# Between two sublayers: the second half's root steps among the first half's features, the last tile's sums behind the next unit's first product

## The reference

```
x = x + 0.5 * rmsnorm(swiglu(rmsnorm(x, g0)), g1)
x = x +       rmsnorm(mixer (rmsnorm(x, g2)), g3)
x = x + 0.5 * rmsnorm(swiglu(rmsnorm(x, g4)), g5)
```

## Time and profile before

| | |
|---|---|
| three runs | 2788.54, 2783.35, 2790.81 us (median 2788.54) |
| profiled execution | 2786.83 us, its span 2785.2 us |
| PE busy | 2673.0 us, 96% |
| DVE / ACT / POOL busy | 1274.3 / 855.1 / 427.5 us |
| chain that ended last | PE 90%, DVE 5% |
| root of half 1 and diagonal, third turn | 1376.60 to 1379.91 us |

### The profile page before, as it was taken

How to read it: one execution, slowest core, us unless ns; L and a number is a source line. 1 busy time by engine, 2 the same in 40 slices (tenths; PEclk the granted TensorE clock), 3 DMA queues, 4 the chain that set the end, 5 groups by cost and what they waited for, 6 DMA issues and landing times.

```text
span 2785.2 us, 52286 instructions
## 1 busy us (share of the span) xinstructions
PE 2673.0 (96%) x20733; PEld 2511.4 (90%) x20733; DVE 1274.3 (46%) x2112; ACT 855.1 (31%) x1415; POOL 427.5 (15%) x616
## 2 busy tenths in 40 slices
PE   7999999999888999999999999999999889999998
PEld 6999998977444999999899999899999878999998
DVE  5444226554544444432444442468435555544423
ACT  2222223233432332222332232334333233322221
POOL 3000003011443100000100000255144442000001
PEclk9999999999999999999999999999989999999999
DMA  4233322222997222332123333133110114233321
GB/s 116 83 90 88 102 75 69 77 68 72 332 339 264 61 83 84 90 103 84 56 85 89 89 97 94 44 84 83 46 36 1 31 47 129 77 89 90 103 84 43
DMA packets 397671, 263.03 MB, mean 94 GB/s; under 512 B 10954, under 2 KB 370583, under 8 KB 397497
## 3 DMA queue, kind: packets, MB, share of 16 engines
q1 hardware_dynamic: 386012, 223.03, 27.4%
q0 software_dynamic: 11536, 38.28, 4.1%
HBM read 251.71 MB, written 9.56 MB: 94 GB/s over the span
## 4 chain that ended last, share of the span: by engine, by line
PE 90%; DVE 5%; issue 1%; ACT 1%; DMA 1%; POOL 1%; SPq 0%; DVEq 0%; POOLq 0%; ACTq 0%
PE ps L486 67%; PE ps L472 5%; PE ps L2247 2%; PE ps L2268 1%; PE ps L1369 1%; PE ps L2265 1%; PE ps L1381 1%; PE ps L1421 1%; PE ps L500 1%; PE ps L1312 1%; PE ps L1330 1%; PE ps L527 1%; PE ps L1313 1%; PE ps L2231 1%; PE ps L2489 1%
## 5 line engine op out<-in xcount | busy, mean ns | idle before, releaser
L464 DVE TENSOR_TENSOR w_lo<-w_raw,w_hi 128x1024 fp32r<-128x1024 f32 (+1 forms) x314 | 419.8, 1337 | 957.9 <-ACT w_hi L457 956.6
L486 PE MATMUL ps<-hd_hi,w_hi 128*128 128x272 f32 x3712 | 774.7, 290 | 6.0 <-DVE w_lo L464 6.0
L486 PE MATMUL ps<-hd_lo,w_hi 128*128 128x272 f32 x3712 | 767.9, 288 | 0.0
L486 PE MATMUL ps<-hd_hi,w_lo 128*128 128x272 f32 x3712 | 764.1, 287 | 0.0
L457 ACT CAST w_hi<-w_raw 128x1024 fp32r<-128x1024 f32 (+1 forms) x314 | 351.1, 1118 | 1088.6 <-PE ps L486 1023.0
L486 PEld LDWEIGHTS ps<-hd_hi,w_hi 128*128 128x128 f32 x3712 | 581.4, 189 | 14.7 <-issue 14.3
L486 PEld LDWEIGHTS ps<-hd_lo,w_hi 128*128 128x128 f32 x3712 | 584.7, 189 | 0.0
L486 PEld LDWEIGHTS ps<-hd_hi,w_lo 128*128 128x128 f32 x3712 | 582.3, 189 | 0.0
L967 POOL TENSOR_TENSOR xT<-xT,rstd_rows 128x272 f32<-128x272 f32 x96 | 81.0, 871 | 1709.4 <-DVE rstd_rows L992 1709.4
L486 PE MATMUL ps<-h_hi,w_hi 128*128 128x272 f32 x1232 | 255.3, 289 | 0.0
L486 PE MATMUL ps<-h_lo,w_hi 128*128 128x272 f32 x1232 | 254.7, 288 | 0.0
(11 more groups left out here) (500 smaller groups left out, 3175.6 us busy)
## 6 DMA issues: line engine op xcount, KB each, us to landing
w_raw<-in_ffn_w_gate_dram SPq DMA_DIRECT2D x88, 512.0 KB, 3.8
w_raw<-in_ffn_w_up_dram SPq DMA_DIRECT2D x88, 512.0 KB, 3.8
w_raw<-in_ffn_w_down_dram SPq DMA_DIRECT2D x64, 704.0 KB, 4.5
k_pages<-in_cache_a_k_dram SPq DMA_DIRECT2D x128, 256.0 KB, 4.6
v_pages<-in_cache_a_v_dram POOLq DMA_DIRECT2D x128, 256.0 KB, 4.5
w_raw<-in_c_w_in_dram SPq DMA_DIRECT2D x33, 512.0 KB, 4.1
w_raw<-in_ab_w_in_dram SPq DMA_DIRECT2D x25, 512.0 KB, 3.9
w_raw<-in_ab_w_out_dram SPq DMA_DIRECT2D x8, 512.0 KB, 3.7
```

Of the source, the lines that this page charges most:

```text
L464: e.tensor_tensor(w_lo[:, n % 2, 0:nk * P], raw[:, n % RAW, 0:nk * P], w_hi[:, n % 2, 0:nk * P].bitcast(F32), ALU.subtract).then_inc(sem(" ...
L486: mm = e.matmul(ps[:, bank + h, 0:TH], w, x[:, k0 + k, half(h)], start=first and k == 0 and w is wh and x is x_hi, stop=last and k == nk - ...
```

## The change

1. `pe_y` ends with its products unless it is the last sublayer. The last sums of half 1, with their wait, become `pe_last_sums`, which `pe_head` of the next sublayer calls right after the three products of feature 0, half 0, of the first unit.
2. `pe_rows` of half 1 moves from behind feature 4 to behind feature 5.
3. ACT does features 2, 3 and 4 of half 0 before it casts the second unit.
4. DVE: the twelve small operations of half 1's root no longer run as one chain at k = 5. `dve_rstd_step` issues them one at a time, four each in k = 2, 3 and 4 of half 0: one before `scaled`, two after it, one after `x_low`. Each but the first waits for the one before it; step 0 waits for `y_summed`. The diagonal follows at k = 5, and the split of the second unit moves from k = 3 to k = 6. This order holds in the last turn too, where `x_low` is absent.

```diff
--- before.py
+++ after.py
@@ -511,9 +511,11 @@
                         if at == 0:
                             e.wait_ge(sem("hd_lo_ready"), base + h * KD + k + 1)
                         mm = pe_passes(e, n, k, hd_hi, hd_lo, k, bank, h, k == 0, k == KD - 1)
+                        if at == 0 and h == 0 and k == 0 and s:
+                            pe_last_sums(e, s - 1)
                         if at == 0 and s:
                             squares(h, k)
-                        if at == 0 and h == 0 and k == 4 and s:
+                        if at == 0 and h == 0 and k == 5 and s:
                             pe_rows(e, s - 1, 1)
                     if h == 1:
                         mm.then_inc(sem("unit_done"), 1)
@@ -529,6 +531,12 @@
                                   skip_group_check=True)
             if last:
                 mm.then_inc(sem("y_summed"), 1)
+
+        def pe_last_sums(e, s):
+
+            g = out_gemm(s)
+            e.wait_ge(sem("y_squared"), y_base[g["name"]] + KD + len(tails_of(g)))
+            pe_sums(e, s, 1, tuple(m % 2 for m in tails_of(g)), False, True)
 
         def pe_first_rows(e):
 
@@ -779,8 +787,8 @@
                     if h == 1:
                         mm.then_inc(sem("unit_done"), 1)
                 mm.then_inc(sem("tail_done"), 1) if h == 0 else None
-            e.wait_ge(sem("y_squared"), y0 + 2 * len(tails_of(g)))
-            pe_sums(e, s, 1, tuple(m % 2 for m in tails_of(g)), False, True)
+            if s + 1 == len(subs):
+                pe_last_sums(e, s)
 
         def act_y(e, g, y, s, pre):
             per, n_end = per_quad(g), g["first"] + 4 * (g["quads"] - 1)
@@ -830,9 +838,11 @@
                 act_pre(e, s + 1, 0, 0, 2)
             e.wait_ge(sem("unit_done"), n_end + 4)
             tail(1)
+            if pre:
+                act_pre(e, s + 1, 0, 2, 5)
             act_split(e, n_end + 5, 0, nk_of(n_end + 5))
             if pre:
-                act_pre(e, s + 1, 0, 2, KD)
+                act_pre(e, s + 1, 0, 5, KD)
                 act_pre(e, s + 1, 1, 0, KD)
 
         def dve_y(e, g, s, new_states=None):
@@ -886,12 +896,40 @@
                 chain(e, e.scalar_tensor_tensor(tmp, tmp, -0.5, x, ALU.mult, ALU.mult))
                 chain(e, e.scalar_tensor_tensor(out, tmp, 1.5, out, ALU.add, ALU.mult))
 
+        def of_rstd_y(h):
+            return (small[:, 6 * x + 3 * h:6 * x + 3 * h + 3] for x in range(3))
+
         def dve_rstd_y(e, s, h):
 
             e.wait_ge(sem("y_summed"), 2 * s + h + 1)
-            mean, r_, tmp = (small[:, 6 * x + 3 * h:6 * x + 3 * h + 3] for x in range(3))
+            mean, r_, tmp = of_rstd_y(h)
             chain(e, e.tensor_scalar(mean, ps[:, 4 + h, 0:3], 1.0 / D_MODEL, EPS, ALU.mult, ALU.add))
             dve_rsqrt(e, r_, tmp, mean)
+            dve_diag(e, r_, h)
+
+        def dve_rstd_step(e, s, x):
+
+            mean, r_, tmp = of_rstd_y(1)
+            if x == 0:
+                e.wait_ge(sem("y_summed"), 2 * s + 2)
+                ins = e.tensor_scalar(mean, ps[:, 5, 0:3], 1.0 / D_MODEL, EPS, ALU.mult, ALU.add)
+            else:
+                e.wait_ge(sem("vector_small"), count["v"])
+            if x == 1:
+                ins = e.tensor_scalar(tmp.bitcast(I32), mean.bitcast(I32), 1, None, ALU.arith_shift_right)
+            if x == 2:
+                ins = e.tensor_scalar(r_.bitcast(I32), tmp.bitcast(I32), -1, MAGIC, ALU.mult, ALU.add)
+            if x >= 3 and x % 3 == 0:
+                ins = e.tensor_tensor(tmp, r_, r_, ALU.mult)
+            if x >= 3 and x % 3 == 1:
+                ins = e.scalar_tensor_tensor(tmp, tmp, -0.5, mean, ALU.mult, ALU.mult)
+            if x >= 3 and x % 3 == 2:
+                ins = e.scalar_tensor_tensor(r_, tmp, 1.5, r_, ALU.add, ALU.mult)
+            count["v"] += 1
+            ins.then_inc(sem("vector_small"), 1)
+
+        def dve_diag(e, r_, h):
+
             diag = strip(6 + h)
             e.tensor_tensor(diag[:, 0:2 * P].rearrange("p (x n) -> p x n", x=2),
                             ident[:, :].unsqueeze(1).to_broadcast([P, 2, P]),
@@ -992,20 +1030,29 @@
                 e.scalar_tensor_tensor(rb[:, half(k % 2)], y[:, k, half(h)], gain(l, n, k), ps[:, 6 + h, 0:TH],
                                        ALU.mult, ALU.mult).then_inc(sem("branch_ready"), 1)
 
+            def step(h, k, x):
+                if h == 0 and 2 <= k < 5:
+                    dve_rstd_step(e, s, 4 * (k - 2) + x)
+
             dve_rstd_y(e, s, 0)
             if pre:
                 dve_split(e, n_next, 0, KD)
             scaled(0, 0)
             for h in range(2):
                 for k in range(KD):
+                    step(h, k, 0)
                     if k < KD - 1:
                         scaled(h, k + 1)
+                    step(h, k, 1)
+                    step(h, k, 2)
                     if pre and k:
                         x_low(e, s + 1, *pre_of(s + 1), h, k - 1)
-                    if h == 0 and k == 3 and pre:
+                    step(h, k, 3)
+                    if h == 0 and k == 5:
+                        e.wait_ge(sem("vector_small"), count["v"])
+                        dve_diag(e, tuple(of_rstd_y(1))[1], 1)
+                    if h == 0 and k == 6 and pre:
                         dve_split(e, n_next + 1, 0, KD)
-                    if h == 0 and k == 5:
-                        dve_rstd_y(e, s, 1)
                 if h == 0:
                     scaled(1, 0)
                 if pre:
```

## The result

The changed kernel took 2793.10 us (median of 20 runs, 2787.93 to 2798.03), the kernel before, on the same chips, 2785.97 (20 runs, 2781.81 to 2790.81). The ratio is 1.0025, 95% interval 1.0019 to 1.0031: +7.0 us, between +5.3 and +8.6. The forecast was 2793.4 with +4.9 on the profiled execution. The absolute time came closer than the step: the median of before in the forecast was that of three runs, 2.6 above that of twenty. The profiled execution after took 2788.50 us, its span 2786.9.

What follows compares the result with a forecast made beforehand. The turn was taken as held by DVE's order up to feature 5, then by PE's slow clock. Five turns +2.3 and the last +2.6 gave +4.9 on the 2788.54 median, 2793.4 us, range 2779 to 2802.

Steps and rivals of the forecast that it cites:

- Step 0 parks 1.8 us: DVE reaches the root's first step at 1370.72 in the third turn and idles until the sums release it at 1372.53.
- Iteration 1.49 + 0.5 of collision = 2.0: On DVE, scaled, low and four steps of one feature take 1.49 us, plus 0.50 held under POOL's add.
- Five collisions a turn at 0.50: POOL's add holds DVE once per iteration and once each at L896 and the weight split, 0.50 us each.
- Half 0 ends 12.5 us behind step 0: The next sublayer's first unit ends half 0 on PE 12.5 us after step 0, in each of five turns.
- The turns +0.2, +1.1, -0.1, +0.2, +0.9: Changes in us of the five turns that lead into a next sublayer, first to fifth; together +2.3.
- the twelve sums at the 2.40 of the earlier trace: Second turn on PE: sums were taken to end 2.40 us after 957.35, at 959.75, giving the turn +1.1.
- The last turn +2.6: With scaled 3 to 6 behind step 0, `scaled(1,0)` comes near 2773.5, +2.6 us on the end; bounds +1.0 and +3.5.
- the costs set at nothing: Early sums on PE worth nothing as feature 1 waits for DVE; ACT's reorder and the later split cost nothing, having cover.
- The sum +4.9: All six turns together: +2.3 us in five and +2.6 in the last, added to the profiled time and the median.
- slow clock in front of B: Rival: half clock on features 6, 7 and the second unit B costs 1.65 us in five turns; +13.1, 2801.6 us; chance 0.17.
- No collisions: Rival: DVE is always first at the port, only POOL waits, iterations take 1.49; -10.2, 2778.3 us; chance 0.16.
- Whole adds: Rival: each DVE collision with POOL's add costs the full add, 0.77 us; +12.5, 2801.0 us; chance 0.07.

Runs made afterwards that it cites:

- e3: e1 with the twelve root steps one feature later (features 3 to 5 instead of 2 to 4) in the inner turns; 2782.26 us, ratio 0.9986.
- e7: e3 with mean and tmp in PSUM, so no step reads two SBUF operands, and the order scaled, low, four steps; 2774.07 us, ratio 0.9954.
- e12: The changed kernel with POOL's adds cut to the first 8 of 272 columns, a price and no version; 2772.05 us, ratio 0.9947.
- e4: e1 with the tmp operand of half 1's root in PSUM instead of SBUF; 2788.2 us, ratio 1.0012.
- e1: The changed kernel with the last turn alone back in the old order, whole root at feature 5; 2790.92 us, ratio 1.0013.
- e8: The kernel before with ACT's edit alone, hi and square of features 2 to 4 ahead of the second unit's cast; 2810.03 us, ratio 1.0073.
- e5: The kernel before with the two PE edits alone, last sums behind feature 0 and row product behind feature 5; 2791.49 us, ratio 1.0014.
- e15: e8 with DVE's weight split moved from k = 3 to k = 6; 2793.64 us, ratio 1.0022.
- e11: e3 with the order scaled, low, four steps, operands left in SBUF; 2782.07 us, ratio 0.9984.

## Why the prediction was right

By its own steps, the third turn moved to after's times (it begins 0.79 us earlier):

- *Step 0 parks 1.8 us.* Foreseen release 1372.53 - 0.79 = 1371.74; measured 1371.75, idle 1.73. e3 shows what the parking cost.
- *Iteration 1.49 + 0.5 of collision = 2.0.* Measured 1.94, 1.94, 1.76. Scaled 4 to 7 foreseen at 1373.91, 1375.91, 1377.76 and 1379.57 (less 0.79), measured at 1373.77, 1375.71, 1377.47 and 1379.27. The 1.49 without collision is what e7 measured.
- *Five collisions a turn at 0.50.* Five found: three steps at +0.59, L937 at +0.50, the split at +0.56. The forecast held a low or L896 in places of them; in the iterations it was the operation next behind the add's start, at the diagonal the second (L937, behind L934 at its usual 0.41). e7 and e12 take the holding away in two ways, and the operations are short again; e4 takes it from two steps, and the low behind them gets it.
- *Half 0 ends 12.5 us behind step 0.* Measured 12.54 in the first and fourth turn, on the path that the forecast has, DVE up to `low(0,6)`, and 12.84 in the third (1384.59 - 1371.75). There it came out by two errors that nearly cancel: DVE was 0.3 us earlier than foreseen, and PE, which I had given back its slow clock, had 6.8 us of it instead of 3.4 and was itself the path from 1375.58 on. The turn had two limits nearly as late as each other; the forecast knew one, so that this one fits to 0.3 us is in part luck.
- *The turns +0.2, +1.1, -0.1, +0.2, +0.9.* Measured +0.25, -0.13, +0.21, +0.27, +1.43. The second is the mis-sized term: I took the twelve sums at the 2.40 of the earlier trace rows, and after they took 1.51 in the chain. The clock had not fallen ahead of them. That term is 0.9 us of the 1.2 by which the turn was missed.
- *The last turn +2.6.* By its own terms it adds up to +2.9: with L899's 0.23 the diagonal ends at 2772.8, not 2772.5. Measured +3.1: three held steps at 0.59 and L937, instead of four at 0.5, and an iteration of 1.66 where 1.57 was foreseen. e1 gives 2.8 of it back.
- Of the costs set at nothing, the ACT edit was so only in company: alone it cost 20 us (e8), and its cover was the split at k = 6 and the early sums. The forecast gave the queue on ACT no price, since it looked only at what the edit takes away. The two edits on PE, also set at nothing, make the first turn 0.83 us longer when they stand alone, by the row product, and the third 0.71 shorter (e5).
- The sum +4.9 stands against +5.1 in the turns and +7.0 in the time. The 1.9 between them lies outside the turns and was not found; the interval reaches down to 5.3. The turns agree the better for misses of opposite sign: -1.2 in the second, and +0.3, +0.1, +0.5 and +0.5 in the third, fourth, fifth and last.

The rivals: "slow clock in front of B" had its condition, a longer slow stretch, but the stretch ended by 1382 and B's half 0 ran in 3.40; e15 shows the case that it meant, with B's 27 products at 4.39 and 4.23 in two turns. "No collisions" was priced at 2778.3; e7, which has none among its steps, and the last turn in the old order, took 2774. "Whole adds" was nearer than I gave it chance: a step behind the add's start is held for all that is left of the add. This is what the Trainium skill states ("SBUF — State Buffer", section "SBUF: two separate sides": the pair is an exclusive lock for the whole instruction), and the trace agrees, held step and add ending 0.03 us apart. The 0.77 a piece was too much only since a step would have taken 0.16 anyway.

## What to carry to other kernels

Small operations laid among large ones are not free where an operation of another engine holds them (0.75 us instead of 0.16 here): look for the operation that starts just behind the neighbour's, and put one there that was not held here, with an operand from PSUM. The order has to go with it (e4), or the next operation is held instead. An operation that waits is put where its wait is already over, and an in-order queue is moved one place at a time, with the first waiter behind each place named. Parts of a change in several queues are not to be priced one by one when one's wait covers another's.

## What the runs showed that was not expected

- Which operations POOL's add (two SBUF inputs, 0.76 us) holds on DVE: both inputs in SBUF (L925 0.75, `low` 0.95), and also a single tensor input, SBUF to SBUF (L921, int32, 128x3, 0.75; L937, 0.73). Not held: PSUM to SBUF (0.16), PSUM and SBUF in (0.17), and scaled, with y in SBUF and the root in PSUM (0.49).
- The other way round, a low of 0.50 that is ahead makes the add 0.97 instead of 0.76.
- PE's clock fell to half in the third turn of the changed kernel behind two microseconds with PE busy 0.28 and 0.36, and stayed at full in the first and fourth turn of e3 and e11 and in e7's first, third and fourth. Over the five turns the 0.50 clock lasts 23.8 us before, 34.0 in the changed kernel, 20.4 in e3 and 13.6 in e7. The edit does not set it alone: with the same code in the five turns, the changed kernel has 3.4 us in the first turn and 6.8 in the fourth, e1 6.8 and 3.4, and all four turns take 24.18 or 24.19. So a slow clock is counted as a cost only where the chain is on PE.
